# Band attention in a streaming encoder layer: factors two units behind their scores, values three

## The reference, cut to what matters

```
def attend(q, k, v, bias, valid):
    s = jnp.einsum('bqhd,bkhd->bhqk', q, k) * (ATT_DH ** -0.5) + bias
    s = jnp.where(valid, s, NEG_INF)
    p = jax.nn.softmax(s, axis=-1)
    return jnp.einsum('bhqk,bkhd->bqhd', p, v)
# 16 heads of 64; each chunk of 64 queries sees its own chunk and the 8 chunks before it
mixed = sigmoid(g_a) * (o_a @ w_branch_gla) + sigmoid(g_b) * (o_b @ w_branch_att)
```

## Time and profile before

| | |
|---|---|
| time, median of 3 runs | 3817.21 us (3809.26 to 3874.46) |
| profiled execution, its own time | 3809.76 us |
| its span on the slowest core | 3808.2 us (all cores: 3793.3 to 3808.2) |
| TensorE matmul busy | 3583.3 us, 94% of the span |
| VectorE, ScalarE, GpSimd busy | 1402.3, 1232.9, 409.7 us |

### The profile page before, as it was taken

One profiled execution on the slowest core, in us unless ns is written; L12 is line 12 of the kernel. 1 busy time (PEld: TensorE's weight loads), 2 busy tenths in 40 slices (PEclk: granted clock), 3 DMA queues, 4 the chain that ended last, 5 costly groups with the idle time before them and its releaser, 6 DMA issues.

```text
span 3808.2 us, 60681 instructions; the slowest of 8 cores (3793.3 to 3808.2 us)
## 1 busy us (share of the span) xinstructions
PE 3583.3 (94%) x20944; PEld 1696.7 (45%) x20944; DVE 1402.3 (37%) x2380; ACT 1232.9 (32%) x2291; POOL 409.7 (11%) x924
## 2 busy tenths in 40 slices
PE   7999999999889999999878999999989999999998
PEld 3444444444344444444443444444434444444443
DVE  2222222222355554546344545463642222222232
ACT  3112111122243635536233354453622221222221
POOL 1032222221000000010100000011010000000000
PEclk9999999999999999999879999999999999999999
DMA  9577768776334334362953443525273111112110
GB/s 183 131 144 167 158 153 176 138 151 155 133 111 155 112 136 142 101 190 78 228 208 122 144 134 111 166 85 180 92 251 114 52 65 62 39 50 67 53 48 26
DMA packets 118505, 477.04 MB, mean 125 GB/s; under 512 B 21999, under 2 KB 22784, under 8 KB 88896
## 3 DMA queue, kind: packets, MB, share of 16 engines
q1 hardware_dynamic: 59520, 328.12, 27.4%
q0 software_dynamic: 58688, 145.04, 17.9%
HBM read 430.96 MB, written 101.97 MB: 140 GB/s over the span
## 4 chain that ended last, share of the span: by engine, by line
PE 81%; DVE 6%; DMA 6%; issue 3%; ACT 2%; POOL 1%; DVEq 0%; SPq 0%; ACTq 0%; POOLq 0%
PE ps L383 76%; DMA s_wring<-wsc 2%; PE ps L1056 2%; DMA s_stg<-wms 2%; PE ps L1011 2%; PE ps L454 1%; DVE s_op L1068 1%; DVE s_va L954 1%; DMA s_vone<-cv 1%; DMA s_nr<-hB 1%; DVE s_oaT L461 1%; DVE s_oa L1233 1%; DVE s_Sf L1196 1%; ACT s_tmpa L1020 1%; PE ps L1080 0%
## 5 line engine op out<-in xcount | busy, mean ns | idle before, releaser
L383 PE MATMUL ps<-s_xnT,s_wring 128*128 128x512 bf16 (+1 forms) x2880 | 630.0, 364 | 47.8 <-DMA s_wring<-wsc 25.4
L383 PE MATMUL ps<-s_xnT,s_w2b 128*128 128x512 bf16 x2816 | 614.1, 380 | 1.5 <-DVE s_xnT L461 1.5
L383 PE MATMUL ps<-s_xnT,s_w1b 128*128 128x512 bf16 x2816 | 614.6, 380 | 0.0
L641 ACT ACTIVATE s_tmpf<-ps 128x512 f32<-128x512 f32 x352 | 209.8, 596 | 1193.1 <-PE ps L383 1193.1
L643 DVE TENSOR_TENSOR s_gT<-ps,s_tmpf 128x512 bf16<-128x512 f32 x352 | 243.5, 692 | 950.8 <-PE ps L383 856.4
L383 PE MATMUL ps<-s_wring,s_xnT 128*128 128x512 bf16 (+1 forms) x1728 | 404.6, 384 | 31.4 <-DVE s_va L954 19.1
L383 PEld LDWEIGHTS ps<-s_xnT,s_w2b 128*128 128x128 bf16 x2816 | 274.4, 98 | 330.0 <-issue 3.8
L383 PEld LDWEIGHTS ps<-s_xnT,s_w1b 128*128 128x128 bf16 x2816 | 274.5, 98 | 328.9 <-issue 3.1
L383 PEld LDWEIGHTS ps<-s_xnT,s_wring 128*128 128x128 bf16 x2880 | 252.6, 101 | 336.1 <-issue 91.8
L383 PE MATMUL ps<-s_w1c,s_gT 128*128 128x512 bf16 x1408 | 311.9, 380 | 0.0
L383 PE MATMUL ps<-s_w2c,s_gT 128*128 128x512 bf16 x1408 | 310.1, 379 | 0.0
(11 more groups left out here) (135 smaller groups left out, 3145.4 us busy)
## 6 DMA issues: line engine op xcount, KB each, us to landing
s_wring<-wsc SPq DMA_DIRECT2D x198, 1024.0 KB, 5.9
s_stg<-wms POOLq DMA_DIRECT2D x88, 256.0 KB, 5.6
wsc<-s_stg POOLq DMA_DIRECT2D x88, 256.0 KB, 4.5
s_stg<-w2s POOLq DMA_DIRECT2D x66, 256.0 KB, 5.7
w2b<-s_stg POOLq DMA_DIRECT2D x66, 256.0 KB, 4.2
s_rring<-xp SPq DMA_DIRECT2D x32, 512.0 KB, 12.6
hA<-s_rring SPq DMA_DIRECT2D x32, 512.0 KB, 8.4
s_hb<-hA SPq DMA_DIRECT2D x8, 2048.0 KB, 13.3
```

What stands on the lines that cost most here:

```text
L383: ins = e.matmul(out_ap, lhsT=l, rhs=r, start=(start and i == 0), stop=(stop and i == n - 1))
L641: S.op("act", (lambda e, b=bg_, tb=tb, T=T: e.activation(out=tmpf[:, tb, 0:T], in_=bank(b)[:, 0:T], func=AF.Silu)), reads=[("ps", bg_)], w ...
```

## The change

Nothing is computed that was not computed before, and every instruction keeps its size. What changes is order, and one buffer:

- `att_fac` comes two units behind `att_sc` instead of one, `att_pv` three instead of two.
- A third staging buffer is used by every third unit. It is `tmpf[:, 1]`, which the wide stream's gates write too. So the wide stream gets a new hold, "att", ahead of the gates; it is lifted after the last factor.
- `op_turn` of a pair stands directly ahead of the first values of the next pair, where it stood one unit later. Ahead of it the wide stream gets an allowance of 2 matmuls more.
- The allowance per unit falls from 130 to 112 matmuls over the loop for a prompt tile, and to 64 for the sample tile, where it was 130 as well.

```diff
+            def stagebuf(u):
+                if u % 3 < 2:
+                    return tmpa[:, u % 3, :, :], ("tmpa", u % 3)
+                return tmpf[:, 1, :].rearrange("p (h n) -> p h n", h=2), ("tmpf", 1)
+
             def att_sc(u):
                 c, g = units[u]
-                pbuf, tb = u % NB, u % 2
+                pbuf = u % NB
+                ta, tkey = stagebuf(u)
...
-            DEPTH = 2
+            DEPTH = 3
             R = len(groups)
 
             def attention():
                 S.enter("Pb")
-                for u in range(len(units) + DEPTH + 2):
+                for u in range(len(units) + DEPTH + 1):
                     if u < len(units):
                         att_sc(u)
                         yield
-                    if 1 <= u <= len(units):
-                        att_fac(u - 1)
-                    if u >= R + DEPTH + 1 and (u - DEPTH - 1) % R == 0:
-                        op_turn((u - DEPTH - 1) // R - 1)
+                    if 2 <= u < len(units) + 2:
+                        att_fac(u - 2)
+                    if u == len(units) + 1:
+                        stream.ready.add("att")
+                    if u >= R + DEPTH and (u - DEPTH) % R == 0:
+                        yield ahead
+                        op_turn((u - DEPTH) // R - 1)
                     if DEPTH <= u < len(units) + DEPTH:
                         att_pv(u - DEPTH)
                     yield tail if u >= len(units) else 1
 
-            step_ = 130.0 / (2 * len(units))
-            tail = 4.0 / step_
+            step_ = (112.0 if kind == "p" else 64.0) / (2 * len(units))
+            tail, ahead = 4.0 / step_, 2.0 / step_
...
             def wide():
                 yield from proj_gla()
                 yield "gla"
+                yield "att"
                 yield from merges()
```

More of the change, by code:

```diff
@@ L1019, in att_sc @@
                 if nb:
-                    S.op("act", lambda e: e.activation(out=tmpa[:nk, tb, :, 0:nb * TP], in_=ps[:nk, b:b + 2, 0:nb * TP], func=AF.Exp, scale=0.125),
-                         reads=[("ps", b), ("ps", b + 1)], writes=[("tmpa", tb)])
+                    S.op("act", lambda e: e.activation(out=ta[:nk, :, 0:nb * TP], in_=ps[:nk, b:b + 2, 0:nb * TP], func=AF.Exp, scale=0.125),
+                         reads=[("ps", b), ("ps", b + 1)], writes=[tkey])
                 if n > nb:
@@ L1036, in att_fac @@
                             out=Pb[:nk, pbuf, :, c0 * TP:(c0 + nb) * TP].rearrange("p h (b q) -> p h b q", b=nb),
-                            in0=tmpa[:nk, tb, :, c0 * TP:(c0 + nb) * TP].rearrange("p h (b q) -> p h b q", b=nb),
+                            in0=ta[:nk, :, c0 * TP:(c0 + nb) * TP].rearrange("p h (b q) -> p h b q", b=nb),
                             in1=biasT[:nk, 2 * c:2 * c + 2, k0:k0 + nb, 0:TP], op=ALU.mult)),
-                            reads=[("tmpa", tb), ("biasT", 2 * c), ("biasT", 2 * c + 1)], writes=[("Pb", pbuf, 1)])
+                            reads=[tkey, ("biasT", 2 * c), ("biasT", 2 * c + 1)], writes=[("Pb", pbuf, 1)])
                     if r <= 3 and r < NS and TP == 128:
```

## The result

The changed kernel takes 1.0106 times the time of before, 95% interval 1.0069 to 1.0143; its runs that count are at 3850, 3852 and 3859 us. (The median of all its runs, 3977 us, contains executions in which one die ran at a lower clock; the ratio leaves such runs out on both sides.) The profiled execution took 3851.69 us, against 3809.76 us before. The forecast was 3798 us, the range 3774 to 3824 us.

The account below looks back on a forecast made before the run. TensorE's matmuls, busy 3583.3 of 3808.2 us, bound the kernel, with 80 us of attention idle to win. Five-group −2, four-group −8 and sample tile −3 make −13 from 3809.8: 3797, forecast 3798 us, range 3774 to 3824.

Parts of the forecast that it names:

- the transposes one unit earlier: Attention, pool "E" banks: moving op's transposes shifts the wide groups' waits; −0.4 us a five-group tile with the chain.
- own-bank starts: Attention: wide group or key transpose waits for evacuation of the group ahead in its bank; 48.0 us before.
- the chain: Closing chain of a pair, five-group tiles: 0.29 us of wait stays at six pairs, now ahead of the transposes.
- −0.4 us a five-group tile: Five-group tiles' attention: idle time 7.0 us after against 7.4 us before; −2 us for six tiles.
- The four-group tiles: Attention of the two four-group tiles: chain waits vanish, own-bank starts shrink; −3.8 us a tile, −8 us for two.
- The sample tile: Sample tile's attention: wide stream spread over all units, the 1.89 us wait for weights goes; −3 us.
- The factor's step: Attention: factor two units behind removes values' waits for factors, 2.9 us; VectorE's wait behind exponentials close to zero.
- The stop of the first value group: Five-group tiles, behind a key transpose: evacuation behind chain and one more factor, 1.52 us becomes 2.1 us.
- the ring transfers: SyncE's queue: transfer issued about 3 us later stays hidden; at most 27 us in all if not.
- Slower: Rival: factors stand ahead of evacuations more often, nine own-bank starts a five-group tile cost 0.60 us more; 3831 us, chance 0.11.
- Deeper gain: Rival: VectorE's 89.8 us behind ScalarE make evacuations late; without them 3758 us at most, or 3770 us; chance 0.12.
- The clock: Rival: even spread holds 2.4 GHz in the sample tile's attention, 7 us more gain; 3790 us, chance 0.06.

Follow-up runs that it names:

- the best kernel: Changed kernel with op transposes one unit later, leftover −2, evacuations at the latest behind the same round's factor; ratio 0.9902 to the kernel before, lowest run 3768 us.
- run 3768: Lowest run of the best kernel: changed kernel with late op transposes, leftover −2 and evacuations behind the same round's factor; 3768 us, ratio 0.9902.
- the kernel with the longest attention: Changed kernel with each GLA projection group's evacuation queued right behind its last piece; ratio 1.0096 to the kernel before.

## Why the prediction was wrong

*The step that failed first is "the transposes one unit earlier".* It asked only on whose bank the wide group behind the transposes falls. It never asked whose bank the transposes themselves take, and so put that wait at nothing. TensorE's waits in the attention of one five-group tile after (slowest core, 1266.8 to 1341.9):

```profile
PE ps L383 <- DVE s_va L954: 3.8, 3, 2.1
PE ps L1087 <- DVE s_kiT L942: 3.0, 2, 1.5
PE ps L1087 <- DVE s_qdT L934: 1.5, 1, 1.5
PE ps L1087 <- DVE s_op L1075: 1.4, 3, 0.7
PE ps L964 <- DVE s_va L954: 1.0, 1, 1.0
```

The terms that the sum had came out well: own-bank starts 3.8 + 1.0 = 4.8 us, forecast 2.1 + 1.1 + 1.6 + 0.5 = 5.3; the chain 1.4 us, forecast 1.7. The term that it lacked is the transposes' wait for a bank, three times 1.5, together 4.5 us. The forecast of −0.4 us a five-group tile became +3.0 to +4.6. The written order of pieces, which agreed with the trace, already held the collision (a piece of a group, then the transposes): it was a missed reading, not a missing row. In 14 of the 48 five-group stretches the clock also falls behind the stop of 2.1 us, and these last 75.1 us instead of 74.1; the forecast had the stop, but no price for the clock behind it.

*The second failure is a term that was not in the sum.* I checked that the allowances end with nearly the same number of matmuls given out, and took what follows for unchanged. The leftover was 2 matmuls different, and the next stage starts from it. It costs 14.5 us of waits for `mixT` (7.6 to 22.1). The rest of the +16.4 us, 2 us, is of the size of the clock. At the stop ahead of the first `oaT` product TensorE stands still for 1.65 to 1.85 us in both kernels, and behind it the granted clock sometimes falls to 1.2 GHz: in the first tile the eight matmuls there took 1.89 us on six of the eight cores before, and over 3 us on seven of the eight after, as here on core 5:

```profile
1164.50 3.57 PE L383 MATMUL ps<-s_oaT,s_wring 128*128 128x512 bf16 x8 [1.66 <-DVE s_oaT L461]
```

The granted clock from 1164.5 to 1168.1 is 0.50 there. On core 5 the second tile of the kernel before has such a place too (3.42 us at 1378.76). Counted over all cores and tiles, the clock falls at 26 of 63 such stops before and at 45 of 60 after, which is 2.6 us more a core. With leftover −2 put back it is 21 of 60, with leftover 0 in the kernel before 47 of 62. So in these four kernels it goes with the leftover. Others do not follow: 24 of 60 with evacuations right behind their pieces and leftover 0, 38 to 44 of 60 to 64 with evacuations behind the factor and leftover −2. Each count is of one execution, and what decides it stays open.

*The four-group tiles.* Forecast −3.8 us each, measured −1.9 and −0.6. In the first of them, on the slowest cores, the waits for the chain fell from 2.5 to 0.7 us and the own-bank starts from 9.9 to 8.5 us, nearly as forecast, but the transposes' bank took 2.1 us of it.

*The sample tile.* Forecast −3 us. The attention piece is 2.0 us shorter, the piece behind it 3.0 us longer, so nothing is left. What lengthens the latter was not tried by itself. By the loop's arithmetic that tile's leftover changed too, from 8 matmuls, of which the loop keeps 4, to −1, and the runs that set the leftover did so in prompt tiles alone.

*Right.* The factor's step: VectorE's wait behind exponentials fell from 89.8 us to 12.9 + 5.7 = 18.6 us, the values' wait for factors is gone, and so is their wait for the chain. It bought next to no time, because TensorE itself had waited there only 2.9 us. The stop of the first value group was forecast at 2.1 us and is 2.13 us. The hold "att" and the ring transfers cost nothing that a run shows: with the two causes put back, hold and lower allowances are still in, and the time is that of before.

*The rivals.* "Slower" came true, with the right mechanism (chain and factor ahead of an evacuation in VectorE's in-order queue), half the size (+21 us, measured +42) and the wrong place: it charged the own-bank starts of wide groups, and the cost fell on the transposes. "Deeper gain" named about the time that the best kernel reached (3758 to 3770, measured 3768), but partly by luck: it took VectorE's waits behind ScalarE for the reason why evacuations are late, and with these waits down to 18.6 us the own-bank waits did not fall. They fell when the evacuations were put elsewhere in the queue, an edit that the change doesn't have. The clock did not rise: 0.982 before, 0.979 after on average of the cores; in the sample tile's attention it was 0.63 to 0.69 before and 0.58 to 0.68 after.

The Trainium skill, page TensorE: Matmul & The Clock Gate, section "A second HAM failure mode: psum-queue depth-cycling", tells of a kernel with bf16 matmuls of 512 columns and PSUM banks cycled each iteration, in which TensorE idles for moments often enough that its clock swings between its two levels. The runs agree with it in part. The sum of the stops does not decide: the kernel with the longest attention, 611.4 us, has no fall of the clock in any prompt tile's attention. The length of a single stop goes with it: every fall there, in every kernel, begins from 0.3 us before to 1.4 us after the end of a stop of 1.6 to 2.5 us. Over the whole kernel little of it shows; the mean granted clock of a core stays between 0.976 and 0.983 in all profiled executions.

## What to carry to other kernels

When an instruction moves in a hand-written order, list every buffer that it takes from a rotating pool and ask where the release of that buffer stands in the other engine's queue, not only what the instruction reads. An evacuation that is put into the queue "when the generator resumes" belongs behind work that is ready and ahead of chains that TensorE waits for; deeper staging paid here only once that was so. And a credit or phase that one stage leaves to the next is part of the change: hold it fixed, or measure it by itself.

## What the runs showed of the hardware that was not expected

Half a piece of phase, 2 matmuls of leftover at the start of the GLA stage, moved the kernel by 0.5% in either direction, in two kernels (1.0049 one way; 1.0106 to 1.0058 the other, where the intervals touch but the runs themselves do not overlap). A wait of 1.66 us was followed by 8 matmuls in 1.89 us on one core and 3.57 us on another, at the same place of the same code.

In the attention of five-group tiles the granted clock fell behind a stop of 2.13 us in 47 and 46 of 48 stretches in two kernels, but in only 14 and 17 of 48 in two others that have the same stop; behind a stop of 1.61 us in 12 and 9 of 48; and not at all in the kernel before, whose longest stops there are 1.53 to 1.74 us, nor in the four kernels with shorter ones. The stop costs its own length, and the fall about 1 to 1.6 us more.
